# Turning V: 32x32 squares by VectorE, squares placed by the loads, a stationary V read with a stride of four elements

## What is computed

```python
proj = x @ w_in
for i in range(nb):                      # blocks of 128 queries, 4 heads of 128
    z = einsum('bhqd,bhnkd->bhqnk', q_blk, k_pre) * scale
    log_1m = where(valid, log_sigmoid(-z), 0.0)
    within, later = ...                  # sums of log_1m over the keys behind
    w = where(valid, exp(log_sigmoid(z) + within + later), 0.0)
    o = einsum('bhqnk,bhnkd->bhqd', w, v_pre)
```

## Time and profile before

| | |
|---|---|
| median of 3 runs | 2305.55 us |
| the profiled execution's own time | 2303.36 us |
| its span, first to last instruction | 2301.6 us |
| TensorE matmul busy | 2283.5 us, 99% of the span |
| TensorE weight load busy (beside the matmuls) | 1887.2 us |
| VectorE busy | 1441.2 us, 63% |
| ScalarE busy | 1060.4 us, 46% |
| GpSimd busy | 1224.2 us, 53% |
| DMA | 297.84 MB in 114419 packets |

### The profile page before, as it was taken

How to read it: one execution, slowest core, us unless ns; L and a number is a source line. 1 busy time by engine, 2 the same in 40 slices (tenths; PEclk the granted TensorE clock), 3 DMA queues, 4 the chain that set the end, 5 groups by cost and what they waited for, 6 DMA issues and landing times.

```text
span 2301.6 us, 29983 instructions
## 1 busy us (share of the span) xinstructions
PE 2283.5 (99%) x10824; PEld 1887.2 (82%) x10824; DVE 1441.2 (63%) x1658; ACT 1060.4 (46%) x1627; POOL 1224.2 (53%) x847
## 2 busy tenths in 40 slices
PE   9999999999999999999999999999999999999998
PEld 6888888888878888888888888888888778878887
DVE  7555552763486477468877777723844595486476
ACT  5555542342484255332576676632342683355220
POOL 1666653864456355435476566644763556345341
PEclk9999999999999999999999999999999999999999
DMA  6544422124343344373344544322133334354442
GB/s 234 188 158 156 145 75 96 55 83 133 108 112 124 133 126 141 109 278 143 107 159 139 166 154 130 118 95 75 55 123 135 85 99 146 128 144 126 145 166 83
DMA packets 114419, 297.84 MB, mean 129 GB/s; under 512 B 11232, under 2 KB 41056, under 8 KB 113248
## 3 DMA queue, kind: packets, MB, share of 16 engines
q1 hardware_dynamic: 112544, 290.68, 38.1%
q10 hardware_dynamic: 1728, 5.24, 0.7%
HBM read 216.19 MB, written 71.30 MB: 125 GB/s over the span
## 4 chain that ended last, share of the span: by engine, by line
PE 96%; issue 2%; DVE 2%; DMA 1%; ACT 0%; DVEq 0%; ACTq 0%
PE J L817 20%; PE J L819 20%; PE J L818 20%; PE AO L989 8%; PE ZZ L989 8%; PE AO L817 2%; PE AO L819 2%; PE AO L818 2%; PE ZZ L819 2%; PE ZZ L818 2%; PE ZZ L817 2%; PE AO L943 1%; PE JX L943 1%; PE ZZ L1024 1%; PE ZZ L912 1%
## 5 line engine op out<-in xcount | busy, mean ns | idle before, releaser
L2326 POOL TENSOR_TENSOR WLS<-SR,WHS 128x512 fp32r<-128x512 f32 x264 | 411.5, 1577 | 109.4 <-ACT WHS L1151 101.6
L817 PE MATMUL J<-XBH,WHS 128*128 128x512 f32 x1152 | 452.3, 393 | 0.0
L819 PE MATMUL J<-XBH,WLS 128*128 128x512 f32 x1152 | 449.1, 390 | 0.0
L818 PE MATMUL J<-XBL,WHS 128*128 128x512 f32 x1152 | 448.8, 390 | 0.0
L817 PE MATMUL J<-XBH,WH 128*128 128x512 f32 x864 | 340.0, 394 | 0.2
L819 PE MATMUL J<-XBH,WL 128*128 128x512 f32 x864 | 337.0, 390 | 0.0
L818 PE MATMUL J<-XBL,WH 128*128 128x512 f32 x864 | 336.7, 390 | 0.0
L2318 POOL TENSOR_TENSOR SR<-RAW 128x512 f32<-128x512 f32 x71 | 106.4, 1498 | 293.0 <-DMA RAW<-w 254.5
L819 PEld LDWEIGHTS J<-XBH,WLS 128*128 128x128 f32 x1152 | 216.3, 188 | 46.0
L817 PEld LDWEIGHTS J<-XBH,WHS 128*128 128x128 f32 x1152 | 216.4, 188 | 43.6 <-DVE XBL L1703 0.2
L818 PEld LDWEIGHTS J<-XBL,WHS 128*128 128x128 f32 x1152 | 216.4, 188 | 43.5 <-issue 0.2
(11 more groups left out here) (298 smaller groups left out, 4751.2 us busy)
## 6 DMA issues: line engine op xcount, KB each, us to landing
RAW<-w SPq DMA_DIRECT2D x144, 512.0 KB, 3.7
pk_m<-MB SPq DMA_DIRECT2D x56, 512.0 KB, 5.1
MB<-pk_m SPq DMA_DIRECT2D x48, 512.0 KB, 4.1
KC<-pk_k SPq DMA_DIRECT2D x40, 512.0 KB, 5.3
VC<-pk_v SPq DMA_DIRECT2D x40, 512.0 KB, 4.4
BRAW<-w SPq DMA_DIRECT2D x64, 256.0 KB, 5.1
XRAW<-xt SPq DMA_DIRECT2D x8, 1024.0 KB, 13.2
pk_v<-STL SPq DMA_DIRECT2D x16, 512.0 KB, 5.0
```

The source lines that it names most:

```text
L817: nc.tensor.matmul(to, wh, xh, start=first, stop=True, skip_group_check=True)
L818: nc.tensor.matmul(to, wh, xl, start=False, stop=True, skip_group_check=True)
L819: return nc.tensor.matmul(to, wl, xh, start=False, stop=True, skip_group_check=True)
L2326: low = G_.tensor_tensor(WLS[:, k, :], SR[:, k, :], WHS[:, k, :].bitcast(F32), ALU.subtract)
```

## The change

- TensorE no longer turns V: `turn` and its 16 groups of four transposes go, and with them two waits on `v_blk`.
- VectorE turns V (`turn_values`, at piece 10 of the odd head pair): two instructions of 128x512, each of which transposes 32x32 squares within the same 32 partitions. The four blocks of 128 keys of a chunk are interleaved in the output, so that each instruction writes with a stride of four elements, 16 bytes. The output goes into the tile where the raw keys were (it waits on `k_kept`).
- ScalarE makes the high part from there in one copy of 128x1024 (`values_hi`), VectorE the rest in one subtraction of 128x1024 at piece 12 (`rest_values`).
- pk_v has a new layout. A store moves 4096 contiguous bytes per partition, where it moved eight runs of 512 bytes.
- `load_v` is four DMAs instead of one, each into a group of 32 partitions, of 8 runs of 512 bytes per partition (128 KB each). They move the squares to their partitions.
- VC is [2, P, BLOCKS] instead of [BLOCKS, 2, P]: `values` reads the stationary block with a stride of four elements instead of contiguously.

```diff
--- before.py
+++ after.py
@@ -228,7 +228,7 @@
         KC = [at(f"KC{i}", R + 48.03125 + 4 * i, [2, C], F32R) for i in range(2)]
         KEEP = at("KEEP", R + 56.03125, [2, C + 2])
         WTL = at("WTL", R + 60.0625, [2, BLOCKS, HALF], F32R)
-        VC = at("VC", R + 68.0625, [BLOCKS, 2, P], F32R)
+        VC = at("VC", R + 68.0625, [2, P, BLOCKS], F32R)
 
 
 
@@ -293,7 +293,7 @@
 
         pk_q = nc.dram_tensor("pk_q", (HALVES, HEADS, P, T), F32).ap()
         pk_k = nc.dram_tensor("pk_k", (HEADS, P, SEQ // C, 2, C), F32).ap()
-        pk_v = nc.dram_tensor("pk_v", (HEADS, P, SEQ // P, 2, P), F32).ap()
+        pk_v = nc.dram_tensor("pk_v", (HEADS, 2, P, SEQ // P, P), F32).ap()
         pk_y = nc.dram_tensor("pk_y", (2, P, T), F32).ap()
         pk_t = nc.dram_tensor("pk_t", (NC, P, C // P * MEM), F32).ap()
         pk_m = nc.dram_tensor("pk_m", (FT, P, T), F32).ap()
@@ -490,8 +490,8 @@
                 half, h = g // PAIRS, g % PAIRS // 2
                 hh = half * HEADS + h
                 for part, of in ((1, places(half, STL)[1]), (0, places(half, STL)[2])):
-                    sp.wait_ge(v_blk, 2 * hh + 2)
-                    sp.dma_start(pk_v[h, :, half * TB:(half + 1) * TB, part, :],
+                    sp.wait_ge(v_blk, hh + 1)
+                    sp.dma_start(pk_v[h, part, :, half * TB:(half + 1) * TB],
                                  of[:].bitcast(F32).rearrange("p (b m) -> p b m", m=P)).then_inc(v_kept[part], 16)
 
             def load_k(half, h, i):
@@ -511,7 +511,10 @@
                     if h == 0:
                         wait_if(sp, o_out[1], 16 * 3 * half)
                 wait_if(sp, pv_done, 2 * n)
-                sp.dma_start(VC[:].bitcast(F32), pk_v[h, :, BLOCKS * (k ^ 1):BLOCKS * (k ^ 1) + BLOCKS]).then_inc(v_in, 16)
+                for q in range(GROUPS):
+                    rows = pk_v[h, :, :, GROUPS * (k ^ 1) + q].rearrange("s (i x) m -> x (s i) m", i=GROUPS)
+                    to = VC[SQUARE * q:SQUARE * (q + 1)].bitcast(F32).rearrange("x s (i r) b -> x (s i) (r b)", i=GROUPS)
+                    sp.dma_start(to, rows).then_inc(v_in, 16)
 
             def piece(g, i):
 
@@ -840,8 +843,6 @@
                 elif i == 0:
                     pe.wait_ge(a_lo, g + 1)
                     wait_if(pe, ad_done, 4 * (g - 1) + 2)
-                    if 2 <= l <= 2 * HEADS and l % 2 == 0:
-                        pe.wait_ge(v_blk, 2 * (half * HEADS + l // 2))
                     if l == 0 and half:
                         pe.wait_ge(row_free, 2 * TB * (half - 1) + 11)
                 elif i == 2:
@@ -869,21 +870,6 @@
                     return
                 if i % 2:
                     mm.then_inc(pr_done, 1)
-                if l < 2 * HEADS and l % 2 and i in (10, 12):
-                    turn(g, 0 if i == 10 else 1)
-
-            def turn(g, part):
-
-                hh = g // PAIRS * HEADS + g % PAIRS // 2
-                v, c = places(g // PAIRS, ST)[2], J[(g + 1) % 2]
-                if part:
-                    pe.wait_ge(v_blk, 2 * hh + 1)
-                else:
-                    pe.wait_ge(ad_done, 4 * g + 2)
-                for j in range(4):
-                    mm = nc.tensor.transpose(c[:, j * P:(j + 1) * P], v[:, (4 * part + j) * P:(4 * part + j + 1) * P],
-                                             IDENT[:])
-                mm.then_inc(v_tr, 1)
 
             def pair(g, inside={}, first=0):
                 for i in range(first, PIECES):
@@ -950,11 +936,11 @@
                 if diag and j == 0:
                     wait_if(pe, y_f, y_count(half, 0, h) + c)
                 pe.wait_ge(wt_lo, 2 * (gp + 1))
-                pe.wait_ge(v_in, 16 * (n + 1))
+                pe.wait_ge(v_in, 16 * GROUPS * (n + 1))
                 blocks = j + 2 if diag else BLOCKS
                 for b in range(blocks):
                     q = P if diag and b == j + 1 else 0
-                    mm = pass3(OB[:, j * P + q:j * P + HALF], (VC[:, BLOCKS - 1 - b, 0, :], VC[:, BLOCKS - 1 - b, 1, :]),
+                    mm = pass3(OB[:, j * P + q:j * P + HALF], (VC[:, 0, :, BLOCKS - 1 - b], VC[:, 1, :, BLOCKS - 1 - b]),
                                (WTH[:, gp % 2, b, q:HALF], WTL[:, gp % 2, b, q:HALF]), diag and j == 0 and b == 0)
                 mm.then_inc(pv_done, 1)
 
@@ -1257,14 +1243,14 @@
                     sums_of(g + 1, False)
                 elif i == 11:
                     shared(g, 1, 0, 0, 6)
-                if g % PAIRS < 2 * HEADS and g % 2 and i in (10, 12):
-                    values_hi(g, 0 if i == 10 else 1)
-
-            def values_hi(g, part):
+                if g % PAIRS < 2 * HEADS and g % 2 and i == 10:
+                    values_hi(g)
+
+            def values_hi(g):
 
                 hh = g // PAIRS * HEADS + g % PAIRS // 2
-                act.wait_ge(v_tr, 2 * hh + part + 1)
-                nc.scalar.copy(places(g // PAIRS, STL)[2][:, part * C:(part + 1) * C], J[(g + 1) % 2][:]).then_inc(v_hi, 1)
+                act.wait_ge(v_tr, NC * (hh + 1))
+                nc.scalar.copy(places(g // PAIRS, STL)[2][:], places(g // PAIRS, ST)[1][:]).then_inc(v_hi, 1)
 
             def split_keys(g):
 
@@ -1735,15 +1721,23 @@
                 d = dest(g)[p][:, c * C:(c + 1) * C]
                 V_.tensor_tensor(d, bank[:], d, ALU.add).then_inc(ad_done, 1)
 
-            def turned(g, part):
+            def turn_values(g):
 
                 hh = g // PAIRS * HEADS + g % PAIRS // 2
-                t = slice(part * C, (part + 1) * C)
-                dve.wait_ge(v_hi, 2 * hh + part + 1)
+                dve.wait_ge(ad_done, 4 * g + 2)
                 dve.wait_ge(k_kept, 32 * (hh + 1))
-                hi, lo = places(g // PAIRS, STL)[2], places(g // PAIRS, STL)[1]
-                V_.tensor_tensor(lo[:, t], J[(g + 1) % 2][:], hi[:, t].bitcast(F32),
-                                 ALU.subtract).then_inc(v_blk, 1)
+                _, to, v = places(g // PAIRS, ST)
+                for c in range(NC):
+                    t = slice(c * C, (c + 1) * C)
+                    V_.transpose(to[:, t].rearrange("p (q x b) -> p b q x", q=GROUPS, b=BLOCKS),
+                                 v[:, t].rearrange("p (b n) -> p b n", b=BLOCKS)).then_inc(v_tr, 1)
+
+            def rest_values(g):
+
+                hh = g // PAIRS * HEADS + g % PAIRS // 2
+                dve.wait_ge(v_hi, hh + 1)
+                _, lo, hi = places(g // PAIRS, STL)
+                V_.tensor_tensor(lo[:], places(g // PAIRS, ST)[1][:], hi[:].bitcast(F32), ALU.subtract).then_inc(v_blk, 1)
 
             def rest_of_first(g, parts=(0, 1)):
                 if g > GLAST:
@@ -1788,8 +1782,10 @@
                     rest_of_first(g + 1)
                 if i == 9 and quiet(g + 1):
                     rest_of_sums(g + 1, False)
-                if l < 2 * HEADS and l % 2 and i in (10, 12):
-                    turned(g, 0 if i == 10 else 1)
+                if l < 2 * HEADS and l % 2 and i == 10:
+                    turn_values(g)
+                if l < 2 * HEADS and l % 2 and i == 12:
+                    rest_values(g)
 
             def pair(g, after={}, first=0):
                 for i in range(first, PIECES):
```

## The result

The changed kernel takes 2393.95 us (median of 4 runs, 2392.96 to 2394.72), the kernel before, measured beside it, 2305.41 us (2305.02 to 2305.99). The ratio is 1.0384, 95% interval 1.0366 to 1.0402: 88.5 us slower. The forecast was 2302.9 us; the third rival, with 2389 us at half rate, is what came true.

What follows compares the result with a forecast made beforehand. TensorE's queue was taken as the path from end to end. The terms -7.5 (transposes) + 0.5 (VectorE) + 4.3 (loads of V) + 0 (stationary loads) = -2.7 us gave 2302.9 us, own range 2301 to 2308, 8-in-10 range 2298 to 2316.

Steps and rivals of the forecast that it cites:

- the third rival: Strided stationary is slow: 864 weight loads in `values`, on the path; 2320 us at a quarter slower, 2389 at half rate; chance 0.21.
- What bounds the kernel: TensorE's queue is the path from end to end; its matmuls are busy for 2283.5 of 2301.6 us.
- The stationary loads: 864 weight loads from VC in `values`, now strided: taken as 0 us, since a load uses about half the possible read rate.
- The upper bound: Stationary loads in `values` at a halved rate: 0.22 instead of 0.12 us each, +86 us over 864 loads.
- the slow stride: The rival that strided weight loads in `values` are slow; it decides for slower from 8 ns a load; chance 0.21.
- Transposes off TensorE: 16 parts of `turn` leave TensorE's queue, 0.45 us each, 7.2 us, plus 0.3 us of waits: -7.5 us.
- VectorE's burst: VectorE's added squares and subtraction, 1.8 us per head, at most 3.1, against QL's 2.1 us to spare: +0.5 us.
- the ends 0 and 3: Lower and upper limits, in us, of the cost forecast for VectorE's added work per head; 0.5 us was taken.
- V's four loads: Loads of V into VC: set complete 5.1 us after issue, so seven short chunks wait 0.2 to 1.0 us: +4.3 us.
- The rival "in time": V's four load parts complete by 4.7 us, chunks wait 1.8 us in all: -5.7 us, 2299.9 us; chance 0.25.
- What would show it: Signs in the profile after: VC wait about 5 us, sets issued over 1.7 us, weight loads 188 ns, products 0.12 us apart.
- the forecast's "no change": Whole kernel: -2.7 us, 0.12% less, within the 0.2% (4.6 us) that a measurement can't tell from no change; chance 0.40.

## Why the prediction was wrong, by its own steps

- **What bounds the kernel** held: TensorE's queue from end to end. Its corollary, no more than 0.01 us of cover for a weight load in `values`, held as well: the products moved from 118 to 234 ns apart.
- **The stationary loads: "I take 0"** is the step that failed. It measured +93.6 us alone (864 products, 93.0 us more from start to start). The upper bound was nearly right: I took 0.22 us for a halved rate, the trace shows 0.235. What failed is the choice between the bounds, made by a comparison of rates: that a load takes 0.86 ns an element and a moving operand 0.45 says what each does with contiguous data, and not that the slower one has time to spare. The run with a strided moving operand shows each of them at half of its own rate. With 864 loads, no cover and no row for the price, a chance of 0.21 for the slow stride was too small.
- **Transposes off TensorE: -7.5 us.** The price of a part was right: the 16 places gained 7.6 us, 0.47 each, where the earlier trace rows gave 0.45. The waits were under-priced: 0.3 us was taken, and the waits on `v_blk` at piece 0 of the next pair, which the earlier trace rows doesn't list, gave back another 0.7 us at two heads. In all about -8.3.
- **VectorE's burst: +0.5 us.** The squares took 1.10 us, the subtraction 1.25. The wait on QL is the forecast's kind (0.6 us, once, under the 1 us named), and its 2.1 us to spare were read rightly. But the forecast looked at QL alone. What VectorE does behind QL comes later as well, up to REST, and there the scores wait again; together the starts of heads lost 3.2 us in the run of the squares alone, outside the ends 0 and 3. With the strided write, ScalarE's later copy added waits on WTL.
- **V's four loads: +4.3 us.** Alone they cost +3.5 us, which looks like a hit and is not: I had seven chunks waiting 0.2 to 1.0 us each, because a set would be complete after 5.1 us. It was complete after 4.29 us, two of the seven waited, and one chunk that was not among them, issued behind a load of weights, took 7.0 us. So the number is luck. The rival "in time" was right about the median.
- **What would show it**: SyncE's sets span 1.8 us at the median, as forecast (1.7); VC's wait is 1.5 us, under the 2 us named as a sign of a wrong forecast; the distance of products grew by 116 ns, where 8 were named.

Without the stride the change measured 2.8 us slower (0.13%): the forecast's "no change", with the other sign. Its profiled execution, matmul by matmul against the one before: -7.6 us at the turns, -0.7 at pieces 0 behind them, +4.5 at the scores at the start of heads, +2.4 at two loads of V, +2.5 at six smaller places, +1.0 at one step in cross-attention, which the change doesn't touch, and the end comes 2.3 us later. Of the smaller ones three are the waits on WTL; what makes the others late was not tried apart.

## What to carry to other kernels

Lay out a TensorE operand so that each 16 bytes of a partition hold at least two elements that are read one after the other: a stride of 2 f32 was nearly free here (120 ns from product to product instead of 118), a stride of 4 doubled the pitch of 256-column products, and that for the stationary and the moving operand alike. When a change puts a new access pattern into hundreds of instructions that have no cover, and no row prices it, the forecast should follow the bound that the count makes large; an argument from the rate of another unit is not a row. And a gain of a few us bought with more DMA issues is paid back in the queue that issues them, or in the tile that they free late. To tell the two apart, follow the wait back through every engine: a queue that runs late in plain sight need not be the one waited for.

## What the runs showed of the hardware

- A stationary or moving f32 operand pays for each 16-byte piece as much as for two elements: 1.83 ns a piece for a weight load (distances of 120, 176 and 234 ns for 64, 96 and 128 pieces of 128 elements; 118 contiguous), 0.91 ns a piece for a moving operand (256 pieces in 233 ns, one stride measured). Stride 8 costs the stationary 8 ns more than stride 4.
- VectorE's write has such a price too: squares of 128x512 took 684 ns written plainly, 1098 with a stride of 16 bytes. The Trainium skill's rule ("Advanced Engine Details and Errata", "SBUF Cachelines") speaks of accesses to SBUF in general, and this agrees. With a stride of 8 bytes two halves of 128x256 took 411 ns each. By the plain squares of 512 and 1024 elements (684 and 1246 ns) a plain one of 256 would take 403 ns, an estimate, so the stride of 8 bytes is nearly free here as well.
- A 512 KB load as four DMAs of 32 partitions was complete after 4.29 us at the median, as one DMA after 4.35, with 1.3 us of issue inside. In the changed kernel it was 4.5. Where another DMA was issued less than 0.8 us ahead, the four took 5.3 to 8.1 us, the one 4.0 to 7.1.
- Eight stores of 128 KB with runs of 128 bytes took 4.9 to 8.3 us of SyncE's time, 0.3 to 2.6 us for one; two stores of 512 KB took 1.0 to 1.1 us with runs of 512 bytes and mostly 0.8 with runs of 4096.
